# Gated linear attention: small-block levels as four 32 by 32 squares per tile

## The reference, cut to what matters

```python
b = jnp.cumsum(logg, axis=3)
...
diff = bc[:, :, :, None, :] - bc[:, :, None, :, :]
decay = jnp.where(mask3, jnp.exp(jnp.where(mask3, diff, 0.0)), 0.0)
att = jnp.einsum('bhik,bhjk,bhijk->bhij', qf, kf, decay)
o_intra = jnp.einsum('bhij,bhjv->bhiv', att, vf)
blast = bc[:, :, -1:, :]
kdec = kf * jnp.exp(blast - bc)
state = jnp.exp(blast[:, :, 0, :])[..., None] * state + jnp.einsum('bhjk,bhjv->bhkv', kdec, vf)
```

## Time and profile before

| what | us |
|---|---|
| median of 3 runs (2109.06 to 2121.23) | 2116.32 |
| the profiled execution | 2114.41 |
| its span, first to last instruction | 2112.7 |

### The profile page before, as it was taken

The page is one execution under the profiler, slowest core; times in us unless marked ns, Lnnn a source line. Parts: engine busy times, 40 slices in busy tenths (PEclk is TensorE's granted clock), DMA queues, the critical chain, the costliest instruction groups (busy, mean ns, idle before and its releaser), DMA issues. The chain is left out here.

```text
span 2112.7 us, 28354 instructions
## 1 busy us (share of the span) xinstructions
PE 2054.5 (97%) x10041; PEld 1663.5 (79%) x10041; DVE 1125.4 (53%) x2013; ACT 817.3 (39%) x1485; POOL 393.6 (19%) x329
## 2 busy tenths in 40 slices
PE   7899999999999999999999999899999999999998
PEld 5678788887878888888878778687878888877787
DVE  7755464636456463635545432686868784334312
ACT  5433443534343342434334411544453534223312
POOL 2323232322323232322310011300101010000011
PEclk9999999999999999999999999999999999999999
DMA  7222212122212222122414420411111111512422
GB/s 246 65 61 61 65 51 70 50 70 54 60 50 60 70 50 65 50 70 55 132 53 171 144 60 20 135 30 39 43 30 50 30 50 40 153 52 90 149 60 100
DMA packets 208840, 155.97 MB, mean 74 GB/s; under 512 B 8378, under 2 KB 196100, under 8 KB 208132
## 3 DMA queue, kind: packets, MB, share of 16 engines
q1 hardware_dynamic: 204384, 149.25, 23.2%
q0 software_dynamic: 3584, 4.48, 1.0%
q10 hardware_dynamic: 804, 1.33, 0.2%
HBM read 130.56 MB, written 24.48 MB: 73 GB/s over the span
## 5 line engine op out<-in xcount | busy, mean ns | idle before, releaser
L288 DVE TENSOR_TENSOR w_lo<-w_raw,w_hi 128x512 fp32r<-128x512 f32 x303 | 268.9, 888 | 343.8 <-ACT w_hi L284 343.1
L284 ACT ACTIVATE w_hi<-w_raw 128x512 fp32r<-128x512 f32 x308 | 192.6, 626 | 225.6 <-PE z_ps L317 105.4
L212 PE MATMUL z_ps<-b_parts,w_hi 128*128 128x512 f32 x680 | 276.2, 406 | 3.4 <-ACT g_gate L222 1.8
L213 PE MATMUL z_ps<-b_parts,w_hi 128*128 128x512 f32 x680 | 270.1, 397 | 0.0
L214 PE MATMUL z_ps<-b_parts,w_lo 128*128 128x512 f32 x680 | 270.1, 397 | 0.0
L315 PE MATMUL z_ps<-ah_hi,w_hi 128*128 128x512 f32 x608 | 246.2, 405 | 5.9 <-ACT qkv L887 4.5
L317 PE MATMUL z_ps<-ah_hi,w_lo 128*128 128x512 f32 x608 | 241.2, 397 | 0.0
L316 PE MATMUL z_ps<-ah_lo,w_hi 128*128 128x512 f32 x608 | 240.7, 396 | 0.0
L212 PEld LDWEIGHTS z_ps<-b_parts,w_hi 128*128 128x128 f32 x680 | 129.3, 190 | 37.4 <-issue 7.6
L214 PEld LDWEIGHTS z_ps<-b_parts,w_lo 128*128 128x128 f32 x680 | 129.2, 190 | 30.6
L213 PEld LDWEIGHTS z_ps<-b_parts,w_hi 128*128 128x128 f32 x680 | 129.5, 190 | 28.9 <-issue 0.5
(11 more groups left out here) (436 smaller groups left out, 3865.6 us busy)
## 6 DMA issues: line engine op xcount, KB each, us to landing
w_raw<-in_a_win SPq DMA_DIRECT2D x220, 256.0 KB, 3.0
w_raw<-in_b_win SPq DMA_DIRECT2D x33, 512.0 KB, 4.0
y_scratch<-y SPq DMA_DIRECT2D x16, 512.0 KB, 2.7
w_raw<-in_a_wout SPq DMA_DIRECT2D x8, 768.0 KB, 5.6
w_raw<-in_b_wout SPq DMA_DIRECT2D x8, 768.0 KB, 5.9
xt_scratch<-xb SPq DMA_DIRECT2D x1, 4096.0 KB, 11.8
y_scratch<-g_gate SPq DMA_DIRECT2D x8, 512.0 KB, 3.8
b_wkv<-in_b_wmem SPq DMA_DIRECT2D x8, 512.0 KB, 6.0
```

The costliest lines, as they stand in the source:

```text
L212: pe.matmul(z_ps[s][:, 0:width], w_hi[slot][:, k, :], hi[k][:, tok], start=(k == 0), stop=False)
L213: pe.matmul(z_ps[s][:, 0:width], w_hi[slot][:, k, :], lo[k][:, tok], start=False, stop=False)
L284: act.activation(op_ring(w_hi, u), op_raw[i], ACT.Copy).then_inc(hi_op, 1)
L288: eng.tensor_tensor(op_ring(w_lo, u), op_raw[i], op_ring(w_hi, u).bitcast(F32), ALU.subtract).then_inc(lo_op, 1)
```

## The change

In `level`, the products of i = 0 and i = 3 to 7 (the diagonal and blocks of up to 32 tokens) are made as four products of 32 keys by 32 queries along the diagonal of each tile, each written to its own 32 partitions and 32 columns of the PSUM area. Levels i = 1 and 2 (blocks of 128 and 64 tokens) stay as they were. The rest of the product area is not written by these levels, and `pick` does not take anything from there.

```diff
                     else:
                         pe.wait_ge(mask_done, (NL + 1) * h + i - 1)
+
+                    size = P if i in (1, 2) else 32
                     for t in range(NT):
-                        tok = slice(t * P, (t + 1) * P)
-                        mm = pe.matmul(dst[:, tok], a[:, tok], c[:, tok], start=True, stop=True)
+                        for g in range(P // size):
+                            tok = slice(t * P + g * size, t * P + (g + 1) * size)
+                            mm = pe.matmul(dst[g * size:(g + 1) * size, tok], a[:, tok], c[:, tok], start=True, stop=True)
                     mm.then_inc(lev_done, 1)
```

## The result

The changed kernel takes 2122.81 us (median of 20 runs, 2114.74 to 2129.74), the kernel before 2116.46 us (20 runs, 2109.06 to 2124.5): a ratio of 1.0031, 95% interval [1.002, 1.0042]. That is +6.3 us where +15.4 was forecast, and no change by the bound of half a per cent. The profiled execution took 2122.36 us, its span 2120.7. A sum that is off by 9 us could pass for a term of the wrong size. The trace shows something else: the levels became 21.5 us shorter, and about 26 us came up in places for which the prediction had no term.

A forecast was written before the change was run, and what follows sets the result against it. TensorE's instruction order was taken as the bound: 64 x 0.032 + 0.38 = 2.43 us a level against 1.79, +0.64 times 24 = +15.4, giving 2129.8; with the profiled execution 1.9 us under the median, 2132 us, range 2106 to 2200.

The forecast's parts named there:

- the bound of half a per cent: Whole kernel: 10.6 us, about what a measurement can tell from no change; a result within it was given 0.16.
- The price of a pair: Squared levels on TensorE: a 32-column load and matmul costs 0.032 us, scaled from 128-column and 512-column widths.
- the lower bound of 0.008: Squared levels on TensorE: least price of a pair in us, if four squares run quite side by side.
- rival (1): Squared levels: a tile's four squares stream at once, level 0.89 us, -22 us, 2095; chance 0.09 (only neighbours overlapped: 2107, 0.10).
- The change of division: Either side of each squared level: switching the array's division loses 0.19 us each way, 0.38 us per level.
- The lower bound of nothing: Change of division might cost zero, because the rows read divide the array's rows and the change divides its columns.
- TensorE's order alone sets the end, nearly one to one: Gated-head stage, 1350 to 1810 us: what a level gains or loses on TensorE reaches the end almost fully.
- VectorE has 136 us free of 460: Gated-head stage: VectorE's slack covers its later picks, so what moves with the levels costs zero.
- Nothing else is edited: Whole kernel: no DMA, semaphore, wait or instruction of another engine changes; no cost was charged.
- rival (4): Clock falls behind squared levels, 1.6 us each; after half the 24, +19 us on the forecast, 2151; chance 0.08.
- slower: Whole kernel: the changed kernel takes longer by more than half a per cent (10.6 us); chance 0.75.

The follow-up runs named there:

- sq_gt: Changed kernel with the squares reordered: all eight tiles' first squares, then all second ones, so neighbours use the same quarter; 2119.06 us in a single execution.
- u_after: Changed kernel with TensorE's loop over heads 1 to 3 written out as straight-line code; 2107.43 us, 0.9952 of the kernel before.
- sq_03567: Changed kernel, loop kept, with level 4 as whole tiles again (squares at 0, 3, 5, 6, 7); 2121.18 us, 1.0027 of the kernel before.
- u_pool: u_after with the gate multiplications of `finish` moved from VectorE to GpSimd; 2108.8 us, 0.9968 of the kernel before.
- u_64: u_after with level 2 as two squares of 64 by 64 per tile; 2109.45 us, 0.9961 of the kernel before.
- sq_34: Kernel before with squares at levels 3 and 4 alone; 2117.73 us, 1.0004 of the kernel before.

## Why the prediction was wrong

**The price of a pair: wrong by a factor of 3.5.** I took 0.032 us from the slope of two widths; it is 0.009, next to the lower bound of 0.008 that stood in the text for squares "quite side by side". The slope is a price for neighbours that use the same part of the array: sq_gt measures 0.027. I argued against side by side from matmuls of full width, which have no free part of the array to run beside; the rows could not speak on it. This is rival (1), to which I gave 0.09. Its level of 0.89 is the measured one (0.90), by two small misses that cancel: 0.51 for the pairs, measured 0.58, and 0.38 for the division, measured 0.32. I set it aside for want of a row and because of the width; neither is evidence against it. The Trainium skill, "TensorE: Matmul & The Clock Gate", Part 3, has column tiles run at once, 2.38 times for three; the runs agree in kind, 0.027 to 0.009 us being three times for four.

**The change of division: right.** 0.38 forecast, 0.32 measured for both ways as what is left of a level beside its pairs, though the rows were of a division of the rows. The lower bound of nothing was too kind. The Trainium skill, "TensorEngine Tiling (Array Packing)", Key Properties, has a change of mode drain TensorE; the 0.32 us agree.

**"TensorE's order alone sets the end, nearly one to one": wrong for levels that get shorter.** The text gave the test itself, a stage that differs by something other than 24 times one level's difference: +4.2 against -21.5. The faulty step is the cover "VectorE has 136 us free of 460", an average over a stage with different limits in it. The same view over the 23.5 us up to slot 10's unit shows 0.08 us free. The third line of the earlier trace rows, three waits of 1.8 us in sum, already named the place: it is short because TensorE and VectorE come there almost together. Where TensorE waits already, a gain ahead of the wait is worth nothing, and so it was: 6.7 us of the 7.1 of levels 3 and 4. For a longer level, which I forecast, that wait would only have vanished; for the rival with a shorter one I had to ask who comes next, and did not.

**The instruction supply: no term at all.** "Nothing else is edited" held for operations, waits and DMAs; the number of instructions in the loop is an edit, and cost 9.2 us in two stalls and the clock's falls behind them. u_after puts a price on both, 15.4 us between the medians of after and u_after. The Trainium skill, "Runtime: NRT & Kernel Launch", Instruction fetch mechanics, states that instructions are prefetched in sequence, and that a taken branch to a place that is not held has its target fetched first. The runs agree: no stall at +384 instructions, 3.5 to 4.6 us at +480 and +576 (6 with the second gap of sq_03567), none in straight-line code.

**The clock: priced right, put in the wrong place.** 1.6 us for a fall of 3.4 us stood in rival (4), 1.63 was measured. But the squares don't bring the fall. It stands behind TensorE's waits of 2.65 us and more at slot 10 (3 of 3 in after, u_after, u_pool and u_64, 2 of 3 in sq_34), behind the stalls at the return (6.8 us each in after and sq_03567, 3.4 in sq_gt), and behind none of the slot-10 waits of 1.8 us or less, with the same squares around. Whether idle time is the whole cause is not shown, since before has falls behind L2447 without any.

**The sign and the size.** The forecast of "slower" came near the time by two errors that cancel: a gain of 21.5 us that I made a loss of 15.4, and 26 us of losses that I did not see. That it came near is luck. Without the return's stall the change is faster, 0.9952 with an interval wholly below 1, though by just under the half per cent that the forecast had set as the bound of no change.

## What to carry to other kernels

Where many narrow products can go to different quarters of the array, write them so that neighbours use different quarters; here that alone is the difference between 2.04 and 0.90 us a level. Before a gain on the busiest engine is counted, look at every short wait on it, and at the busy time of the engine behind that wait in the stretch just ahead of it, not over the stage; the gain is worth the slack there and no more. Count instructions in loop bodies: here each return cost microseconds past some length, and writing the loop out took that away at no cost in time.

## What was not expected of the hardware

- Pairs of an f32 load and matmul of 32 columns start 0.009 us apart when they take turns over the four quarters, 0.027 us when they stay in one.
- A loop of TensorE that is returned to twice cost nothing with a body of 384 instructions above the first (about 1510 loads and matmuls: 853 and 852 from 1537.0 to 1649.9 us, one round of after, less 192), and 3.5 to 4.6 us a return with 480 and 576 above it. Straight-line code was fetched in about as many packets (14 against 16) without a stall.
- f32 subtractions of 512 columns on VectorE took 1.78 instead of 0.68 us beside GpSimd's multiplications.
